# First units' sums by column halves, products of two steps up front, and four places for modulation rows

## The reference

```python
cond = jax.nn.silu(c)
for l in range(DEPTH):
    mod = (cond @ w_ada[l] + b_ada[l]).reshape(b, 9, d)     # shift, scale, gate for three sub-layers
    h = modulate(x, mod[:, 0], mod[:, 1])                   # x * (1 + scale) + shift
    x = post_norm_residual(x, swiglu(h, w_ffn_in[l, 0], w_ffn_out[l, 0]), mod[:, 2], 0.5, ln_g[l, 0], ln_b[l, 0])
    ...                                                     # attention with mod 3..5, FFN with mod 6..8
def swiglu(h, w_in, w_out):
    g, u = jnp.split(h @ w_in, 2, axis=-1)                  # w_in 1024 x 5632, w_out 2816 x 1024
    return (jax.nn.silu(g) * u) @ w_out
```

## Time and profile before

| | |
|---|---|
| median of 3 runs | 1059.79 us (1058.85 to 1062.68) |
| the profiled execution | 1057.72 us |
| its span | 1055.9 us |
| TensorE, VectorE, ScalarE, POOL busy | 1017.1, 775.5, 521.4, 85.7 us |
| mean DMA rate | 252 GB/s |

### The profile page before, as it was taken

One profiled execution on the slowest core, in us unless ns is written; L12 is line 12 of the kernel. 1 busy time (PEld: TensorE's weight loads), 2 busy tenths in 40 slices (PEclk: granted clock), 3 DMA queues, 4 the chain that ended last, 5 costly groups with the idle time before them and its releaser, 6 DMA issues.

```text
span 1055.9 us, 12357 instructions
## 1 busy us (share of the span) xinstructions
PE 1017.1 (96%) x4708; PEld 826.3 (78%) x4708; DVE 775.5 (73%) x908; ACT 521.4 (49%) x852; POOL 85.7 (8%) x160
## 2 busy tenths in 40 slices
PE   3799999999999999999999999999999899999997
PEld 1588888878888878888778888888878778888885
DVE  7677777788875888777877587777779777645475
ACT  1545444556564744544464644544468655434432
POOL 0011111101000011111100011111110010000010
PEclk9899999999999999999999999999999999999999
DMA  9999899965785399989937499999846638556551
GB/s 362 349 302 328 299 327 294 333 214 178 264 275 161 108 354 314 316 293 310 326 131 251 146 332 317 310 300 318 312 158 224 203 119 279 166 193 195 181 184 40
DMA packets 147490, 265.61 MB, mean 252 GB/s; under 512 B 8424, under 2 KB 98920, under 8 KB 147432
## 3 DMA queue, kind: packets, MB, share of 16 engines
q1 hardware_dynamic: 124448, 182.87, 51.1%
q0 software_dynamic: 20928, 75.53, 21.0%
q10 hardware_dynamic: 2056, 6.42, 2.0%
HBM read 263.75 MB, written 1.05 MB: 251 GB/s over the span
## 4 chain that ended last, share of the span: by engine, by line
PE 70%; DVE 17%; DMA 5%; ACT 4%; issue 3%; DVEq 0%; SPq 0%; ACTq 0%
PE psum L1251 14%; PE psum L1253 14%; PE psum L1252 14%; PE psum L1328 7%; PE psum L1326 7%; PE psum L1327 7%; DVE w_lo L838 5%; DVE acc L870 5%; DMA ada<-in_w_ada 4%; PE psum L1359 1%; PE psum L1286 1%; ACT psum L594 1%; ACT w_hi L504 1%; PE psum L1273 1%; DVE qT L980 1%
## 5 line engine op out<-in xcount | busy, mean ns | idle before, releaser
L838 DVE TENSOR_TENSOR w_lo<-raw,w_hi 128x2048 fp32r<-128x2048 f32 x164 | 371.5, 2285 | 45.0 <-ACT w_hi L504 44.9
L1251 PE MATMUL psum<-w_hi,hT_hi 128*128 128x512 f32 x896 | 356.0, 397 | 4.3 <-DVE w_lo L838 4.1
L1253 PE MATMUL psum<-w_hi,hT_lo 128*128 128x512 f32 x896 | 350.0, 391 | 0.0
L1252 PE MATMUL psum<-w_lo,hT_hi 128*128 128x512 f32 x896 | 349.0, 390 | 0.0
L504 ACT ACTIVATE w_hi<-raw 128x2048 fp32r<-128x2048 f32 x164 | 310.5, 1915 | 0.0
L508 ACT ACTIVATE tmp<-psum 128x256 f32<-128x256 f32 x88 | 33.8, 384 | 345.8 <-PE psum L1253 345.8
L1251 PEld LDWEIGHTS psum<-w_hi,hT_hi 128*128 128x128 f32 x896 | 168.2, 188 | 40.3 <-DVE w_lo L838 4.0
L1253 PEld LDWEIGHTS psum<-w_hi,hT_lo 128*128 128x128 f32 x896 | 168.2, 188 | 36.0
L1252 PEld LDWEIGHTS psum<-w_lo,hT_hi 128*128 128x128 f32 x896 | 168.5, 188 | 32.9
L870 DVE SCALAR_TENSOR_TENSOR acc<-ada,cond,acc 128x1024 f32<-128x1024 f32 x128 | 164.1, 1282 | 39.8 <-DMA ada<-in_w_ada 30.2
L1326 PE MATMUL psum<-w_hi,a_hi 128*128 128x512 f32 x368 | 150.5, 409 | 0.0
(11 more groups left out here) (151 smaller groups left out, 706.0 us busy)
## 6 DMA issues: line engine op xcount, KB each, us to landing
raw<-in_w_ffn_in SPq DMA_DIRECT2D x176, 512.0 KB, 5.2
ada<-in_w_ada POOLq DMA_DIRECT2D x128, 512.0 KB, 5.2
raw<-in_w_ffn_out SPq DMA_DIRECT2D x88, 512.0 KB, 5.8
raw<-in_w_qkv_a SPq DMA_DIRECT2D x24, 512.0 KB, 5.0
raw<-in_w_o SPq DMA_DIRECT2D x16, 512.0 KB, 4.7
ada<-in_w_kv_ada POOLq DMA_DIRECT2D x16, 512.0 KB, 5.0
raw<-in_w_kv_b SPq DMA_DIRECT2D x16, 512.0 KB, 6.2
raw<-in_w_ada SPq DMA_DIRECT2D x4, 1024.0 KB, 14.0
```

Of the source, the lines that this page charges most:

```text
L838: nc.vector.tensor_tensor(lo_of(n), slot_of(n), hi_of(n).bitcast(F32), ALU.subtract)\
L1251: nc.tensor.matmul(dst, s_hi, m_hi, start=start, stop=False)
L1252: nc.tensor.matmul(dst, s_hi, m_lo, start=False, stop=False)
L1253: return nc.tensor.matmul(dst, s_lo, m_hi, start=False, stop=stop)
```

## The change

The sums of units 0 and 1 are taken in two halves of the columns. A piece (`staged(m)`) now holds four rows of 512 columns. In each half VectorE sums some pieces (3; then 5, 6 and 7), and TensorE sums the others by matmuls whose stationary side is the data and whose moving side is one column of `cond` (pieces 0, 1 and 2; then 4). It adds VectorE's sums with a column of ones (`sum_start`). The result lies in PSUM as a column for each k-tile already, so no unit is turned and ScalarE keeps nothing; `start_coefficients(half)` reads it. When the first half is there, `h` of k-tiles 0 to 3 is computed and the products of steps 0 and 1 over these k-tiles are made (`half_tile`, both token tiles), and those over k-tiles 4 to 7 when the second half is there. The first four chunks are numbered anew for this. Rows of modulation units have four places (two of `ada` and two of `qT`, which is `z`), except for two of the gate units. A unit is turned before the inner transposes of its step, and in such steps tile 0's inner transposes lie in `gu[0]`. The spread of the gate of norm 4 is moved behind the first output products.

```diff
-START_PRODUCTS = (24, 24)
+START_PRODUCTS = (12, 10, 12, 10)
...
+def row_places():
+    loads, last, found = [0] * 4, [0] * 4, {}
+    for u in range(2, UNITS):
+        for row in range(8):
+            p = row % (2 if u in (GATE_OF[1], GATE_OF[4]) else 4)
+            loads[p] += 1
+            found[u, row] = (p, loads[p], last[p])
+            last[p] = 8 * u + row + 1
+    return found
...
+        ada_rows = [ada[:, 0, :], ada[:, 1, :], z[:, 0, :], z[:, 1, :]]
...
+            load_staged(0)
+            load_staged(1)
+            sp.dma_start(cst[:, 0:P], consts[:, 0:P]).then_inc(cst_in, 16)
+            load_x(0)
+            load_first(0)
+            load_staged(2)
+            load_x(1)
+            load_staged(3)
+            load_first(1)
+            load_staged(4)
+            load_staged(5)
+            load_staged(6)
+            load_first(2)
+            load_staged(7)
+            load_first(3)
...
+            def half_tile(s, t, half):
+                n = IN_PAIR[0][s]
+                pe.wait_ge(w_lo_ready, half_of(n, half) + 1)
+                for k in range(4 * half, 4 * half + 4):
+                    if k % 2 == 0:
+                        pe.wait_ge(h_lo_ready, split_count(0, t, k // 2))
+                    last = three(step_bank(0, s, t), h_tok(k, t), w_half(n, k), k == 0, k == KT - 1)
...
+            def sum_staged(m, dst, first):
+                pe.wait_ge(staged_in[m], 16)
+                for r in range(4):
+                    row = 4 * (m % 2) + r
+                    for k in range(4):
+                        last = nc.tensor.matmul(dst[:, k:k + 1], staged(m)[:, r, k * P:(k + 1) * P],
+                                                cond[:, row:row + 1], start=first and r == 0 and k == 0, stop=True,
+                                                skip_group_check=True)
+                last.then_inc(staged_used, 1)
+
+            def sum_start(sums, dst):
+                for k in range(4):
+                    last = nc.tensor.matmul(dst[:, k:k + 1], sums[:, k * P:(k + 1) * P], one[:, :],
+                                            start=False, stop=True, skip_group_check=True)
+                return last
+
+            def add_nothing(times):
+                for _ in range(times):
+                    nc.tensor.matmul(misc[1], zeros[:, 0:P], zeros[:, :], start=False, stop=False,
+                                     skip_group_check=True)
...
+                    if unit_turned(f, s):
+
+                        inner_done(f, s - 1, 1)
+                        turn_unit(first_unit + s // 2 - 1)
                     turn_inner(f, s, 0)
...
-                if h == HEADS:
-
-                    pe.wait_ge(head_kept, 16)
-                    spread_gate(4)
...
             output_rows(1, 0)
+
+            pe.wait_ge(head_kept, 16)
+            spread_gate(4)
             output_rows(1, 1, (0,))
```

More of the change, by code:

```diff
@@ L100, in kept @@
 def kept(u):
-    return sum(v not in GATE_OF for v in range(u + 1))
+    return sum(v not in GATE_OF for v in range(2, u + 1))
 FIRST_UNIT = [unit(0, 3), unit(KV, 0), unit(1, 3), None]
-START_PRODUCTS = (24, 24)
+START_PRODUCTS = (12, 10, 12, 10)
 GATE_W = [0.5, 1.0, 0.5, 0.5, 1.0, 0.5]
@@ L134, in tile_count, with half_of @@
     return 2 * pairs.index(n) + t + 1
+def half_of(n, half):
+    return n + (2 if n < 2 else 1) * half
 def out_chunk(f, s):
@@ L372, in load_ffn @@
                     for half in range(2):
-                        load(n + half, inner_chunk(slot_of(n + half), w_in, 256 * s, half))
+                        if n > 1:
+                            load(n + half, inner_chunk(slot_of(n + half), w_in, 256 * s, half))
                     if s:
@@ L643, in _ @@
             nc.scalar.activation(rowsT[:, :], misc[1][:, 0:256], ACT.Copy).then_inc(rows_ready, 1)
-            keep_unit(0, KT // 2)
-            keep_unit(1, KT // 2)
-            for t in range(TT):
-                h_tile(0, t)
-                split_hi(t)
+            split_hi(0)
+            for half in range(2):
+                for t in range(TT):
+                    h_half(0, t, half)
+                if half == 0:
+                    split_hi(1)
+                    split_hi(2)
+            split_hi(3)
             ffn(0)
@@ L861, in accumulate @@
                         if u not in GATE_OF:
-                            nc.vector.tensor_scalar(sums, src[:, r, :], factor, None, ALU.mult).then_inc(acc_steps, 1)
+                            nc.vector.tensor_scalar(acc[:, :], part, factor, None, ALU.mult)\
+                              .then_inc(acc_steps, 1)
                             continue
@@ L868, in accumulate, with start_coefficients @@
                         dve.wait_ge(acc_steps, 8 * u + 2 * q + r)
-                        base = sums
-                    nc.vector.scalar_tensor_tensor(out=sums, in0=src[:, r, :], scalar=factor, in1=base,
+                        base = acc[:, :]
+                    nc.vector.scalar_tensor_tensor(out=acc[:, :], in0=part, scalar=factor, in1=base,
                                                    op0=ALU.mult, op1=ALU.add).then_inc(acc_steps, 1)
+            def start_coefficients(half):
+                dve.wait_ge(start_sums, half + 1)
+                cols, sums = slice(4 * half, 4 * half + 4), misc[0] if half == 0 else y[2]
+                nc.vector.tensor_tensor(coef[:, 0, 1, cols], sums[:, 0:4], biasT[:, BIAS_AT[0], cols], ALU.add)
+                nc.vector.tensor_tensor(coef[:, 0, 0, cols], sums[:, 8:12], coef[:, 0, 0, cols], ALU.add)\
+                  .then_inc(coef_ready, 1)
             def coefficients(i):
@@ L1280, in turn_x, with turn_unit @@
                 last.then_inc(turned, 2)
-            def turn_unit(u, sums=acc):
+            def turn_unit(u):
                 pe.wait_ge(acc_steps, 8 * u + 8)
@@ L1398, in ffn @@
                     inner_done(f, s - 1, 1)
-                    if first_unit is not None and s % 2 == 0:
-                        inner_done(f, s, 0)
-                        turn_unit(first_unit + s // 2 - 1)
                     add_rows(o, inner(s - 1), 1, first=s == 1).then_inc(w_used, 1)
```

341 lines of the change are left out of this document (222 added, 119 removed).

## The result

The changed kernel takes 1070.09 us (median of 5 runs, 1066.89 to 1070.23), the kernel before 1059.79 (5 runs, 1057.14 to 1062.68). The ratio is 1.0093, 95% interval 1.007 to 1.0115: slower by 0.9%, about 10 us. The forecast was 1052.8, faster, and the time lies above its range of 1046 to 1063. The profiled execution took 1069.94 us, its span is 1068.1.

The account below looks back on a forecast made before the run. The kernel was taken as 43.6 us of start, then TensorE at its own pace. Gains of 4.2 (start), 1.4 (buffers) and 1.7 (gate), less 0.3, made 7.0 us: 1057.7 - 7.0 + 2.1 = 1052.8, range 1046 to 1063.

Parts of the forecast that it names:

- the price of a one-column pass: TensorE's sums at the start: each pass costs its load's spacing, 0.087 us at the half clock, 0.06 at the full one.
- the sum for the coefficients: Start of the kernel: TensorE's queue added up until the first coefficients, 27.6 against 32.17 before, 4.6 us earlier.
- sets 0 and 1: TensorE's first one-column sums at the start: 64 passes at 0.087 us, at the half clock, 5.6 us.
- 12 zero products: TensorE's queue at the start, ahead of set 2: three of them slow, then the clock rises, 3.2 us.
- set 2: TensorE's one-column sums behind the 12 zero products: 32 passes at 0.06 us, 1.9 us.
- The sign that the prediction named for being wrong: At the start: the forecast is wrong if TensorE is still in sets 0 and 1 at 20.
- the slow rival: Start: one-column sums hold TensorE's queue, a pass costing 0.217 us at half clock, 0.11 at full; 1065.5 us, chance 0.16.
- the two waits: TensorE before the turn of unit 2: 1.0 us for `w_lo` of chunk 6, 1.9 us at the turn.
- VectorE's backlog: VectorE from 53.9 to 79.6: five splits, four quarters, nine operations and a 1.7 us wait; unit 2 turned at 79.6.
- Four buffers: Second FFN: rows asked for a quarter earlier, so the unit's turn no longer waits; 1.4 us gained, elsewhere nothing.
- The gate of norm 4: Spread moved behind 24 output products: costs 1.8 instead of 5.2 us, but 1.6 us of waiting for VectorE; 1.7 gained.
- A load has a floor: Rival at the start: a one-column pass costs 0.11 us at either clock, giving 1058.7 us; chance 0.27.

Follow-up runs that it names:

- the first experiment: The kernel before, with groups of small matmuls of several shapes ahead of TensorE's first instruction, at rest and again behind 32 zero products: 1072.23 us, only its trace used.
- the version with both changes: The changed kernel with pieces 0, 1 and 2 summed on VectorE, zero products moved, and remaining one-column matmuls made as two over 64 stationary columns: 1050.73 us, ratio 0.9913.
- the last experiment: The kernel before, with groups of one-column float32 matmuls over 64 and 32 stationary columns ahead of TensorE's first instruction: 0.107 us a 64-column pass to the same half, low clock.
- the version with half loads: The changed kernel, all sets on TensorE, with each matmul of a set made as two over 64 stationary columns: 1054.97 us, ratio 0.9962.

## Why the prediction was wrong

**The step that failed is the price of a one-column pass:** "The moving side is a single column, so I take the load's spacing: 0.087 and 0.06 us." It measured 0.214 at the low clock and 0.106 to 0.112 at the high one. The upper end that I gave, "0.217", was right; it had been read from the transposes, which load 128 columns of float32 as the sets do. The row that I preferred was the wrong neighbour: two loads of 48 rows, and a spacing worked out by taking a mean length from a total. The transposes that belong to those loads stood 0.35 us apart as a pair (14.78 to 15.13 in the trace of before, 0.175 each), twice the spacing that I took from their loads. "The transposes move 128 columns, these one" was the argument against the dear price, and the first experiment shows it empty: up to 128 moving columns the price is the same.

Going through the sum for the coefficients, 27.6 forecast and 42.45 measured (14.85 late):

| term | forecast | measured |
|---|---|---|
| start of the queue | 11.0 | 11.42 |
| sets 0 and 1 | 5.6 | 13.67 |
| eight transposes | 1.7 | 1.74 |
| 12 zero products | 3.2 | 4.52 |
| set 2 | 1.9 | 4.14 |
| eight transposes | 1.0 | 1.74 |
| 10 zero products | 2.2 | 4.01 |
| adding up, coefficients | 1.0 | 1.21 |

The sets make 10.3 us of it, nearly all by the price of a pass. A second step, that the clock rises early in the twelve zero products and stays, makes 3.9 more: nine or ten of the twelve ran at the low level before it rose near 30.9, it fell again at 34.2 among the passes of set 2 (which costs set 2 some 0.6 of its 4.14), and the transposes and nearly all of the ten ran at a clock of 0.50 to 0.53. The sign that the prediction named for being wrong came true: TensorE was in sets 0 and 1 until 25.09.

From the coefficients to the second half's first product it was 24.8 us against 20.5: set 4 took 3.5 instead of 1.9, and the 24 products behind it 7.2 instead of 5.5, at a clock of 0.76. "If the clock falls during set 4, sixteen products after it are slow: 3 us at most" was part of the slow rival, and right in kind (1.7). The two sums took 0.81 each, not 0.5. VectorE's twelve rows took 8.8 us (49.74 to 58.55) and not 7.7: rows of 512 columns come 0.78 us apart, more than half of 1.30. This was hidden here and counts in the version with both changes.

From there to the turn of unit 2 it was 31.7 us (67.23 to 98.96) against 31.5 forecast, with the two waits of 1.3 and 1.6 us forecast as 1.0 and 1.9. The working of the later stages was sound but for one sum: VectorE's backlog from 53.9 on, with the prices given (five times 2.2, four times 2.6, nine times 0.35, and 1.7), ends at 80.2 and not at 79.6. So the start is 15.2 us slower and not 4.2 faster: 14.85 from the coefficients, 4.3 behind them, 0.2 later, less roundings.

**The later parts were right.** Four buffers: forecast 1.4, measured 1.6 (the distance between the kernels goes from 15.21 to 13.64 across the second FFN), by the mechanism named: unit (KV,0) is turned without a wait. No wait of VectorE for rows is left there, and the turn, at 403.90, has no idle time ahead of it. Across the third FFN another 0.4 us is gained (13.64 to 13.26), where the forecast had nothing.

The gate of norm 4: forecast 1.7, measured 1.1. Up to the first output products 2.9 us are gained (836.40 before, 846.80 now, a distance of 10.40), and the spread behind them costs 1.8 (12.18), as forecast. TensorE's wait for VectorE, which I had named and put at 1.6, is 1.96 us:

```profile
844.29 0.70 PE L1806 MATMUL psum<-gate,cst 128*128 128x256 f32 x2 [1.96 <-DVE gate L1358]
```

**The rivals.** "The one-column sums hold TensorE's queue" is what happened: its 1065.5 us, 1068.5 with the falling clock, against 1070.1. For the coefficients it gives 37.9 (27.6, 8.3, and 2.0 for set 2 and the adding) against 42.45; it missed the low clock in the zero products, the transposes and a part of set 2. "A load has a floor", at 0.11 us for either clock, is half right: 0.11 is the price at the high clock, and it doubles at the low one. I gave the slow rival 0.16, although both of its prices came from rows with the same load of 128 float32 columns, one at each clock; what spoke for it, a cost in cycles, was named and not weighed.

**What stays open:** why the clock falls under one-column matmuls that leave no gap. The runs show that it falls among passes over 128 columns and, in the last experiment, over 32. Behind the 64-column sets that ran at the high clock (set 2 of the version with half loads, set 4 of that one and of the one with both changes) the next instructions run at the high clock too; but these sets last only 2 us, so whether narrow loads hold it or are merely over sooner is not shown.

## What to carry to other kernels

Price a small matmul by its stationary side, in its own type and at both clocks, from a row with the same load: a float32 pass over 128 columns was as dear with one moving column as with 128. Work that is moved to an engine "because it waits anyway" stands in that engine's queue ahead of what is urgent; add up the queue from the first instruction at the low clock before the wait is called free. And where one-column products are needed, passes over 64 stationary columns to alternate halves of the partitions cost here about a quarter of a full pass each, so the same sums took half the time. In this kernel that came to 15 us.

## What the hardware showed unexpectedly

- A float32 pass over 128 stationary columns takes 0.213 us at the low clock and 0.112 at the high one, the same with 1, 64 and 128 moving columns.
- Over 64 columns it is 0.107 and 0.058; in turn to both halves, 0.053 and 0.029 (in the sets 0.054 and 0.031, with the hand-overs). Two half passes are cheaper than one whole: a set at the low clock takes 3.43 us with them against 6.84.
- TensorE, busy without a gap, lost the high clock in the middle of one-column float32 matmuls: a set begun behind 28 zero products took 4.62 us, and the next 6.83, where set 4 at the high clock took 3.49. The same happened at 19.35 among passes over 32 columns.
